# Two by two block products for two of every three feed-forward pairs

## The reference, cut to what matters

```python
def _swiglu(x, w_gate, w_up, w_down):        # D_FF = 2816
    return (jax.nn.silu(x @ w_gate) * (x @ w_up)) @ w_down
```

```python
def conv_ffn(h, w_up, conv_w, conv_b, w_down):
    a, b = jnp.split(h @ w_up, 2, axis=-1)
    a = sum(a_pad[:, j:j + T] * conv_w[j] for j in range(3)) + conv_b
    return (jax.nn.silu(a) * b) @ w_down
```

## Time and profile before

| | |
|---|---|
| median of 3 runs | 3392.28 us (3392.01 to 3398.23) |
| the profiled execution | 3394.41 us, of which 3392.6 us is the span |
| PE busy | 3294.0 us, 97% of the span |
| DVE busy | 2160.8 us, 64% |
| ACT busy | 1459.6 us, 43% |
| POOL busy | 345.6 us, 10% |

### The profile page before, as it was taken

How to read it: one execution, slowest core, us unless ns; L and a number is a source line. 1 busy time by engine, 2 the same in 40 slices (tenths; PEclk the granted TensorE clock), 3 DMA queues, 4 the chain that set the end, 5 groups by cost and what they waited for, 6 DMA issues and landing times. The chain is left out here.

```text
span 3392.6 us, 55337 instructions
## 1 busy us (share of the span) xinstructions
PE 3294.0 (97%) x23324; PEld 2795.8 (82%) x23324; DVE 2160.8 (64%) x3230; ACT 1459.6 (43%) x2125; POOL 345.6 (10%) x285
## 2 busy tenths in 40 slices
PE   8999999999999999999999999989999998999998
PEld 6888879688898989878878898877889876678897
DVE  7556565676566656555577466557858664778585
ACT  5333456743344424355654243435424342643242
POOL 1000315400000000042600000010000001400000
PEclk9999999999999999999999999999999999999999
DMA  3232320032323232321022222412222241032222
GB/s 132 89 104 93 111 79 6 24 106 94 110 89 105 92 101 98 100 94 33 16 81 100 100 100 82 131 62 89 94 97 100 87 166 46 14 102 90 101 96 85
DMA packets 57847, 296.85 MB, mean 87 GB/s; under 512 B 6400, under 2 KB 7296, under 8 KB 40064
## 3 DMA queue, kind: packets, MB, share of 16 engines
q1 hardware_dynamic: 57600, 293.31, 25.8%
HBM read 291.19 MB, written 2.10 MB: 86 GB/s over the span
## 5 line engine op out<-in xcount | busy, mean ns | idle before, releaser
L528 ACT ACTIVATE tile_hi<-raw_tiles 128x1024 fp32r<-128x1024 f32 (+3 forms) x353 | 489.3, 1386 | 505.4 <-PE bank L446 429.9
L592 DVE TENSOR_TENSOR tile_lo<-raw_tiles,tile_hi 128x1024 fp32r<-128x1024 f32 (+3 forms) x353 | 582.7, 1651 | 147.3 <-ACT tile_hi L528 138.4
L444 PE MATMUL bank<-hid_hi,tile_hi 128*128 128x512 f32 x1312 | 510.9, 389 | 0.2
L445 PE MATMUL bank<-hid_lo,tile_hi 128*128 128x512 f32 x1312 | 510.5, 389 | 0.0
L446 PE MATMUL bank<-hid_hi,tile_lo 128*128 128x512 f32 x1312 | 510.4, 389 | 0.0
L465 PE MATMUL bank<-src_hi,tile_hi 128*128 128x512 f32 x1152 | 453.7, 394 | 11.3 <-DVE src_lo L1011 5.3
L466 PE MATMUL bank<-src_lo,tile_hi 128*128 128x512 f32 x1152 | 449.9, 391 | 0.0
L467 PE MATMUL bank<-src_hi,tile_lo 128*128 128x512 f32 x1152 | 449.3, 390 | 0.0
L444 PEld LDWEIGHTS bank<-hid_hi,tile_hi 128*128 128x128 f32 x1312 | 246.3, 188 | 54.6 <-DVE tile_lo L592 3.5
L446 PEld LDWEIGHTS bank<-hid_hi,tile_lo 128*128 128x128 f32 x1312 | 246.3, 188 | 51.3
L445 PEld LDWEIGHTS bank<-hid_lo,tile_hi 128*128 128x128 f32 x1312 | 246.3, 188 | 50.5
(11 more groups left out here) (405 smaller groups left out, 6419.8 us busy)
## 6 DMA issues: line engine op xcount, KB each, us to landing
raw_tiles<-in_gu SPq DMA_DIRECT2D x131, 1024.0 KB, 4.9
raw_tiles<-in_down SPq DMA_DIRECT2D x96, 704.0 KB, 4.0
raw_tiles<-in_w_in SPq DMA_DIRECT2D x46, 512.0 KB, 3.5
raw_tiles<-in_a_in SPq DMA_DIRECT2D x17, 512.0 KB, 3.5
raw_tiles<-in_w_out SPq DMA_DIRECT2D x16, 512.0 KB, 3.6
raw_tiles<-in_w_mem SPq DMA_DIRECT2D x16, 512.0 KB, 3.5
masks<-in_masks SPq DMA_DIRECT2D x16, 487.0 KB, 4.5
raw_tiles<-in_b_in SPq DMA_DIRECT2D x9, 512.0 KB, 3.6
```

Of the source, the lines that this page charges most:

```text
L444: nc.tensor.matmul(bank, wh, hi[:, c, 0:p.n], start=(c == 0), stop=False)
L445: nc.tensor.matmul(bank, wh, lo[:, c, 0:p.n], start=False, stop=False)
L528: nc.scalar.activation(self.tile_hi[:, u % 2, 0:width(u)], self.tile_raw[:, u % R, 0:width(u)], ACT.Copy).then_inc(hi_ready, 1)
L592: v.tensor_tensor(self.tile_lo[:, u % R, 0:width(u)], self.tile_raw[:, u % R, 0:width(u)], self.tile_hi[:, u % 2, 0:width(u)].bitcast(F32) ...
```

## The change

Two of every three pairs are in blocks, in all six feed-forward parts: pairs 3, 4, 6, 7, 9, 10 of the first part (5, 6, 8, 9 in the opening feed-forward and in the two with the convolution) and pairs 0, 1, 3, 4, 6, 7, 9, 10 of the second. Two pairs in blocks may now follow each other. The sums of weight blocks no longer have four fixed places: they go round a ring of five (`sum_place`), each sum is split by itself (128x512) instead of two at a time, and PE waits for each of the four before the product that uses it. Where unit u and unit u+1 are both in blocks ("joined"), DVE makes the first sum of u+1 at the start of unit u, the second after PE's product 4, the fourth after PE's product 5, and then the low part of the tile and of the last three sums, behind the gate's scaling and its convolution. Where the first pair in blocks is 5, the sums of the input are made one per pair beside pairs 0 to 3.

In the opening, the first half of the weight tile is loaded ahead of x, the squares are kept in eight places (in the room of the hidden results), half of them are made after the opening loop, DVE adds them (`open_sum`) instead of POOL, the sum of squares product goes behind the gate product of pair 1, and the split of tile 2 is moved ahead into unit 0. The rest is what these need (counters of semaphores, `squares_before`, `turned_at` in `turns_hi` and `make_turns`).

```diff
+    def turned_at(self, i):
+        if self.kind != "gated" or not self.normed:
+            return ()
+        step = 1 if self.blocked[0] > KD // 2 else 2
+        return tuple(range(step * i, min(step * (i + 1), KD // 2)))
...
-EARLY_BLOCKED, LATE_BLOCKED = (3, 5, 7, 9), (0, 2, 4, 6, 8, 10)
-
-
-def feed_forward(up, down, layer, factor, next_gain, taps=None, tap_bias=None):
+EARLY_BLOCKED, OPEN_BLOCKED, LATE_BLOCKED = (3, 4, 6, 7, 9, 10), (5, 6, 8, 9), (0, 1, 3, 4, 6, 7, 9, 10)
+CONV_EARLY_BLOCKED, CONV_LATE_BLOCKED = (5, 6, 8, 9), (0, 1, 3, 4, 6, 7, 9, 10)
+RING = 5
+
+
+def feed_forward(up, down, layer, factor, next_gain, taps=None, tap_bias=None, opens=False):
 
     half = KF // 2
     out = []
     for part in range(2):
-        blocked = LATE_BLOCKED if part else EARLY_BLOCKED
+        if taps is not None:
+            blocked = CONV_LATE_BLOCKED if part else CONV_EARLY_BLOCKED
+        else:
+            blocked = LATE_BLOCKED if part else OPEN_BLOCKED if opens else EARLY_BLOCKED
...
-    AT_HID = AT_SUM + SLOT
+    AT_SUM = AT_SUM_HI + RING * QUARTER
+    AT_HID = AT_SUM + RING * QUARTER
...
-        assert not any(in_blocks(u) and in_blocks(u + 1) for u in range(last))
...
-                if source == "x":
-                    self.open_squares(pool, own)
...
-                        if i == 0 and p.normed and (blocks[0] == 0) != opens:
+                        if blocks[0] == 0 and p.normed and i == (1 if u < 2 and source == "x" else 0):
...
-                    pe.wait_ge(sum_split, 2 * s + 1)
+                    pe.wait_ge(sum_split, 4 * s + 1)
                     product(carried, combined, 0, lambda j: turn(j, 3), True).then_inc(multiplied, 1)
                     pe.wait_ge(tile_split, u + 1)
                     product(first_bank, straight, 0, lambda j: source(j, 0), True).then_inc(multiplied, 1)
                     product(single[0], straight, 1, lambda j: source(4 + j, 0), True).then_inc(multiplied, 1)
                     pe.wait_ge(kept, 4 * s + 1)
+                    pe.wait_ge(sum_split, 4 * s + 2)
                     product(carried, combined, 1, lambda j: source(4 + j, 1), False).then_inc(multiplied, 1)
-                    pe.wait_ge(sum_split, 2 * s + 2)
+                    pe.wait_ge(sum_split, 4 * s + 3)
                     pe.wait_ge(kept, 4 * s + 2)
                     product(first_bank, combined, 2, lambda j: turn(j, 0), False).then_inc(multiplied, 1)
                     pe.wait_ge(read_out, 2 * s + 1)
                     product(single[1], straight, 2, lambda j: turn(j, 2), True).then_inc(multiplied, 1)
                     pe.wait_ge(read_out, 2 * s + 2)
+                    pe.wait_ge(sum_split, 4 * s + 4)
...
-                def split_sums_hi(u):
-                    for half in range(2):
-                        act.wait_ge(added_up, 4 * nth(u) + 3 + half)
-                        at = slice(2 * half * QUARTER, 2 * (half + 1) * QUARTER)
-                        nc.scalar.activation(self.sum_hi[:, at], self.sum_raw[:, at], ACT.Copy).then_inc(sum_hi_ready, 1)
+                def split_sum_hi(u, k):
+                    act.wait_ge(added_up, 4 * nth(u) + (1, 3, 2, 4)[k])
+                    nc.scalar.activation(self.sum_place(self.sum_hi, nth(u), k), self.sum_place(self.sum_raw, nth(u), k), ACT.Copy).then_inc(sum_hi_ready, 1)
...
+                    if u < last and not (source == "x" and u == 1):
                         split_hi(u + 1)
                     if p.in_blocks(i):
                         self.keep_carried(act, own, u, p, i)
                         if is_pair(u - 1):
                             self.hidden_hi(act, own, *units[u - 1])
+                        if in_blocks(u + 1):
+                            split_sum_hi(u + 1, 0)
                         self.keep_first(act, own, u, p, i)
-                        self.keep_late(act, own, u, p, i)
+                        self.keep_late(act, own, u, p, i, 0)
+                        if in_blocks(u + 1):
+                            split_sum_hi(u + 1, 1)
+                            split_sum_hi(u + 1, 2)
+                        self.keep_late(act, own, u, p, i, 1)
+                        if in_blocks(u + 1):
+                            split_sum_hi(u + 1, 3)
...
-                def split_sums_lo(u, half):
-                    if in_blocks(u):
-                        at = slice(2 * half * QUARTER, 2 * (half + 1) * QUARTER)
-                        dve.wait_ge(sum_hi_ready, 2 * nth(u) + half + 1)
-                        v.tensor_tensor(self.sum_lo[:, at], self.sum_raw[:, at], self.sum_hi[:, at].bitcast(F32),
-                                        ALU.subtract).then_inc(sum_split, 1)
+                def split_sums_lo(u, ks):
+                    for k in ks if in_blocks(u) else ():
+                        lo, raw, hi = (self.sum_place(at, nth(u), k) for at in (self.sum_lo, self.sum_raw, self.sum_hi))
+                        dve.wait_ge(sum_hi_ready, 4 * nth(u) + k + 1)
+                        v.tensor_tensor(lo, raw, hi.bitcast(F32), ALU.subtract).then_inc(sum_split, 1)
+
+                def add_weights(u, steps):
+                    for k in steps if in_blocks(u) else ():
+                        self.add_weight(dve, own, landed[u % R], u, *units[u], k)
...
-                    if in_blocks(u + 1):
-                        self.add_weights(dve, own, landed[(u + 1) % R], u + 1, *units[u + 1])
-                    if u < last:
+                    joined = in_blocks(u) and in_blocks(u + 1)
+                    add_weights(u + 1, (0,) if joined else range(4))
+                    if u < last and not joined and not (source == "x" and u == 1):
                         split_lo(u + 1)
+                    if source == "x" and u == 0:
+                        self.open_sum(dve, own)
                     if is_pair(u - 1):
                         self.hidden_lo(dve, own, *units[u - 1])
                     if p.in_blocks(i):
                         self.first_half(dve, own, u, p, i)
+                        if joined:
+                            add_weights(u + 1, (1,))
+                            split_sums_lo(u + 1, (0,))
+                            add_weights(u + 1, (2,))
                         self.scale_gate(dve, own, u, p, i)
+                        if joined:
+                            add_weights(u + 1, (3,))
+                            split_lo(u + 1)
+                            split_sums_lo(u + 1, (1, 2, 3))
                         continue
                     if p.kind == "gated":
-                        if p.normed and i < 2:
+                        if p.turned_at(i):
                             self.make_turns(dve, own, p, i)
-                        split_sums_lo(u + 1, 0)
-                        split_sums_lo(u + 1, 1)
+                        if source == "x" and u == 0:
+                            split_lo(2)
+                        split_sums_lo(u + 1, range(4))
...
-    def add_weights(self, dve, own, landed, u, p, i):
-
-        v, s, R = self.nc.vector, self.nth_blocked[p.pairs + i], self.SLOTS
-        added_up = own["added_up"]
+    def sum_place(self, at, s, k):
+
+        return at[:, (4 * s + k) % RING, :]
+
+    def add_weight(self, dve, own, landed, u, p, i, step):
+
+        v, s, R, added_up = self.nc.vector, self.nth_blocked[p.pairs + i], self.SLOTS, own["added_up"]
         raw = lambda block: self.tile_raw[:, u % R, block * QUARTER:(block + 1) * QUARTER]
-        total = lambda block: self.sum_raw[:, block * QUARTER:(block + 1) * QUARTER]
-        dve.wait_ge(landed, 16 * (u // R + 1))
-        if p.normed and i == p.blocked[0]:
-            dve.wait_ge(own["turned"], p.turns + KD // 2)
-        if s:
-            dve.wait_ge(own["multiplied"], self.before_blocked(s - 1) + 1)
-        v.tensor_tensor(total(0), raw(3), raw(2), ALU.add).then_inc(added_up, 1)
-        if s:
-            dve.wait_ge(own["multiplied"], self.before_blocked(s - 1) + 5)
-        dve.wait_ge(added_up, 4 * s + 1)
-        v.tensor_tensor(total(2), total(0), raw(0), ALU.subtract).then_inc(added_up, 1)
-        dve.wait_ge(added_up, 4 * s + 2)
-        v.tensor_tensor(total(1), raw(1), total(2), ALU.subtract).then_inc(added_up, 1)
-        if s:
-            dve.wait_ge(own["unit_done"], self.unit_blocked[s - 1] + 1)
-        v.tensor_tensor(total(3), raw(0), raw(3), ALU.subtract).then_inc(added_up, 1)
+        total = lambda k: self.sum_place(self.sum_raw, s, k)
+        if step == 0:
+            dve.wait_ge(landed, 16 * (u // R + 1))
+            if p.normed and i == p.blocked[0]:
+                dve.wait_ge(own["turned"], p.turns + KD // 2)
+            if s >= 2:
+                dve.wait_ge(own["unit_done"], self.unit_blocked[s - 2] + 1)
+            v.tensor_tensor(total(0), raw(3), raw(2), ALU.add).then_inc(added_up, 1)
+        if step == 1:
+            if s:
+                dve.wait_ge(own["multiplied"], self.before_blocked(s - 1) + 4)
```

(81 more changed lines are left out.)

25 lines of the change are left out of this document (12 added, 13 removed).

## The result

| | before | after |
|---|---|---|
| median of 4 runs | 3393.55 us (3392.01 to 3398.23) | 3420.5 us (3418.03 to 3427.76) |
| ratio, 95% interval | | 1.0077 (1.0064 to 1.009) |
| the profiled execution | 3394.41 us, span 3392.6 us | 3418.03 us, span 3416.2 us |

The changed kernel is 0.77% slower. PE does 648 more but shorter matmuls and is busy 12.4 us less (before: the earlier trace rows); DVE is busy 108.2 us more. The first two lines are the page after; under them stand its groups of PE's wait for the tile's low part and of the splits of sums (line, engine, output and input, count, busy, mean ns, idle before and releaser).

The account below looks back on a forecast made before the run. PE bounds the kernel on average, DVE the convolution stages. Opening -7.5, plain +2, convolution +25, slow clock +5.5 make +25 us on 3394.4, less 2.1 for the median: 3417 us; own range 3403 to 3431, 8 in 10 within 3392 to 3432.

Parts of the forecast that it names:

- PE saves 0.84 us per pair in blocks: Any pair turned into blocks: 10.07 us on PE for 10.91; 18 more such pairs, 15 us less if nothing waits.
- Plain parts, +2 us: Feed-forward parts without convolution: PE 0.7 us late in each joined pair before a straight one, so the saving returns as waiting.
- Convolution, +25 us: Two feed-forwards with the convolution: DVE's load loses 2.1 us in each of 12 joined pairs, bounds +6 to +34.
- The new wait for `hid_hi`: DVE's loop in the convolution parts: a new wait of 1.0 us, as only one sum stands before `hid_lo`.
- The stall in front of the first pair in blocks: Convolution parts, before pair 5: the 2.92 us idle is not saved; 2.2 us stay and the rest come back in that pair.
- Slow clock, +5.5 us: After half of the 12 new convolution stalls PE runs slow, 0.9 us each; bounds 0 and 11.
- Opening, -7.5 us: Opening feed-forward: without POOL's adding DVE's chain is faster, pair 5 starts at 71.8 us for 79.88; bounds -3 and -10.
- Quarters, 0.13 us per pair: Splitting sums as four of 512 columns costs DVE 0.13 us more per pair; the page's figure gives 0.31.
- Rival (a): Whole kernel: columns decide, DVE catches up in the straight pair, 3359 us; milder form 3374; together chance 0.11.
- Rival (b): Convolution parts: losses half as large, 12 x 1.0 us and no slow clock, 3399 us; chance 0.12.
- Rival (c): Every new stall drops the clock and the plain stalls reach 1 us: 3429 us; chance 0.20.

Follow-up runs that it names:

- e3: The changed kernel, with `first_half` of the second of two joined pairs made before `hid_lo` of the pair before, not behind it; 3407.63 us, ratio to before 1.0042.
- e2: The changed kernel without the convolution's three taps, so the gate is scaled by one DVE instruction in place of four; 3377.67 us.
- e5: The changed kernel with one of the three convolution taps left out, so three scaling instructions in place of four; 3399.99 us.
- o1: The changed kernel, but POOL instead of DVE adds the squares of the opening; 3417.06 us.
- o2: The changed kernel with the opening's old load order, chunks 0 and 1 of x ahead of the half tile; 3424.95 us.
- e1: The changed kernel with the old pattern of pairs in blocks in the two feed-forward parts with the convolution, all else as changed; 3390.76 us in one run.
- e4: e3 with fewer pairs in blocks in the convolution parts (8, 10 and 0, 3, 5, 8, 10), none joined there; 3368.34 us, ratio to before 0.993.

## Why the prediction was right, step by step

The forecast was 3417 us; after has 3420.5. The direction and the place are shown; two sizes were off, and that the total is near is luck: a term that I did not have makes up for them.

- **PE saves 0.84 us per pair in blocks.** Right: 10.07 for 10.91 us, unchanged.
- **Plain parts, +2 us.** Measured +1.0. The second joined pair takes 10.77 us (predicted 10.8), the last one 10.09 (10.2), first parts -0.26 (-0.1) and second parts +0.35 to +0.70 (+0.6). (Added up exactly, the prediction's terms are -0.2 and +0.5, in all +1.4 and not +2.) e3 shows the cause that I gave: `first_half` stands behind the split and `hid_lo`. With it moved, the second parts are 1.45 us shorter than before, so the 0.7 us was order, not load. I had priced it and not seen that it was free to mend.
- **Convolution, +25 us.** Right in kind and nearly in size. The three pairs take 33.84 us (predicted 34.2, before 32.0), the stall is in front of product 2, DVE is 90% busy. Without the slow clock the four parts lost 24.5 - 1.7 = 22.8 us. e2 and e5 show that it is DVE's work: the pair follows the scaling instructions one for one. The new wait for `hid_hi` is there at 0.77 us (I had 1.0). The stall in front of the first pair in blocks stays, 2.07 us before pair 5 and 2.26 us in it, as the prediction said; e2 has neither, e5 only 0.9 us in the pair.
- **Slow clock, +5.5 us.** The weakest term. In the profile after 2 of the 12 stalls were followed by it, at 0.83 us each, 1.7 us; in o1 by 4, in e3 and o2 by 6, as I had assumed. Over these four executions it is 18 of 48, under my half, and the one profiled had few. What decides it between two stalls of equal length the runs don't show.
- **Opening, -7.5 us.** Measured -7.6: pair 1 at 24.49 (25.4), pair 2 at 38.58 (39.1), pair 5 at 71.4 (71.8). Its reason holds in part: the prediction gave DVE's time without POOL nearly all. Of the 7.6 us o1 gives back 1.3 and o2 3.1, of which 1.6 are clock. A term I did not have is the clock before: up to 15.55 - 12.72 = 2.8 us in pair 0 above (part of it may lie under the waits for chunks), and pair 3 took 11.46 us at a granted clock of 0.87 where 10.07 is a pair in blocks, 1.4 us. What is left (the sum of squares behind pair 1, the split of tile 2 moved ahead) was not taken apart.
- **Quarters, 0.13 us per pair.** Shown by e1. VectorE: DVE Perf Modes in the Trainium skill (section on the TRN2 errata) has a fixed part in each instruction, from which I had estimated 0.31 us. Its duration agrees (0.69 us for 512 columns), but what counts behind a queue is the step, 0.60 us, and the page's figure would have put e1's pair at 10.71 us, where 10.53 was measured.
- **Not in the sum: +5.7 us in the mixers, which the change does not touch.** The largest piece lies between the last plain part and the first one with the convolution. Its windows before, after and in e1:

```profile
2058.86:2350.36 291.50, 275.60 (x1558) 227.41 (x1557) 169.67 (x299) 116.31 (x179) 15.22 (x16) 0.99 0.29 93
```

```profile
2053.68:2348.84 295.16, 276.99 (x1559) 228.20 (x1557) 169.08 (x299) 116.14 (x179) 15.74 (x16) 0.98 0.30 92
```

```profile
2051.60:2341.83 290.23, 272.57 (x1559) 224.59 (x1557) 169.28 (x299) 116.17 (x179) 15.74 (x16) 1.00 0.30 94
```

The instructions are the same in number to one; PE is busy 275.60, 276.99 and 272.57 us at a granted clock of 0.99, 0.98 and 1.00, and stands still 15.90, 18.17 and 17.66 us. Between e1 and after 4.4 of the 4.9 us are busy time and go with the clock. Between before and after only 1.4 of the 3.7 us are; the rest is waiting, 4.7 us for low parts of tiles in place of 1.7. Why slow stretches and waits fall so in one execution stays open. Over all untouched stretches e1 to e5 stand 0.5, 2.1, 6.3, 2.4 and 5.3 us above before, o1 and o2 1.8 and 4.8, with the same instructions there: a scatter as large as the term itself. The convolution and its slow clock came in 6.0 us below my sum, and these 5.7 us filled it: the profiled executions differ by 23.6 us (predicted 25), the medians by 27.0. So the total agrees better than its terms do.

Rival (a), that the columns decide, is refuted by e4: five pairs in blocks fewer per pair of parts, and 17 us faster. Rival (b), half the loss, is refuted by the pair of 12.86 us. Rival (c), every stall followed by the slow clock, did not come about, though e3 and o2 went half the way.

## What to carry to other kernels

A form that saves the busiest engine time is worth it only where the next engine has room for its price in the same stretch: here 0.84 us saved on PE, for 12.2 us of DVE (the prediction's count) in a pair that PE is through with in 10.07. Work out the load of the second engine stage by stage and choose the form for each stage, instead of one pattern for all (e4: 10 fewer pairs in blocks than e3, and 39 us, 1.2%, faster). And when a stall is found by arithmetic ahead of time, look at the order of the instructions in front of it first: moving one 0.4 us instruction gave back 1.2 to 1.8 us per plain part.

## What was not expected of the hardware

- With POOL adding beside it, each short DVE instruction takes about a microsecond more, with one input or two: 0.42 to 1.51 (256 columns), 0.48 to 1.52 (512, one tensor input) in o1, 0.69 to 1.77 before. The split of 2048 columns that began just before POOL's next add was not longer (2.28 us for 2.30 alone). The GPSIMD Engine Reference in the Trainium skill (Specifications, the row on SBUF interfaces) names contention for DVE instructions with two SBUF inputs or in a two-port mode; the two-input rows agree, and the scaling, with one tensor input and a per-partition scalar, slows as well. Alone, the next instruction starts 0.40 us after a scaling of 512 columns and 0.60 us after a `tensor_tensor` of 512, so the scaling runs at a higher rate; whether that mode is why POOL slows it, no run here shows.
- Of stalls of the same 1.86 us some are followed by 1.2 GHz and some are not, 2 to 6 of 12 in one execution; those of 1.07 us never were (12 in e5). Four more such stretches are 3.3 us in the changed kernel and 5.7 us in e3, and the 4 runs of the changed kernel lie 9.7 us apart; so single runs are read here by their pairs and not by their totals.
